# Half of a query projection moved among the first attention heads, rotation by head pairs, and two conditioning chunks moved to GpSimd

## The reference

```python
mod = c_act @ ada_w + ada_b                       # 1024 x 6144 for each layer
sh1, sc1, g1, sh2, sc2, g2 = jnp.split(mod, 6, axis=-1)
h = modulate(rmsnorm(x, n1), sh1, sc1)
x = x + g1 * mixer(h)                             # layer 0: retention, layer 1: attention
h = modulate(rmsnorm(x, n2), sh2, sc2)
x = x + g2 * f(h)                                 # layer 0: SwiGLU, layer 1: experts
```

```python
proj = h @ w_qkv
q = axial_rope(rmsnorm(q, q_norm_g)); k = axial_rope(rmsnorm(k, k_norm_g))
o = softmax(q @ k.T * 128 ** -0.5) @ v            # per head
m = o @ w_out
```

## Time and profile before

| what | us |
|---|---|
| median of 3 runs | 1654.36 (1654.05 to 1655.42) |
| the profiled execution | 1656.82 |
| its span, first to last instruction | 1654.6 |
| TensorE busy in the span | 1563.3 |
| VectorE busy | 1362.7 |
| ScalarE busy | 978.9 |
| GpSimd busy | 151.7 |
| attention, from the last copied norm to the output projection's end | about 512 to 620 |
| expert passes | about 644 to 1654 |

### The profile page before, as it was taken

One profiled execution on the slowest core, in us unless ns is written; L12 is line 12 of the kernel. 1 busy time (PEld: TensorE's weight loads), 2 busy tenths in 40 slices (PEclk: granted clock), 3 DMA queues, 4 the chain that ended last, 5 costly groups with the idle time before them and its releaser, 6 DMA issues.

```text
span 1654.6 us, 20642 instructions
## 1 busy us (share of the span) xinstructions
PE 1563.3 (94%) x6848; PEld 1248.5 (75%) x6848; DVE 1362.7 (82%) x1076; ACT 978.9 (59%) x790; POOL 151.7 (9%) x146
## 2 busy tenths in 40 slices
PE   5999779899997689999999999999999999999996
PEld 4677547677776568887888888888888888888885
DVE  6799478877767767888888888888888888888987
ACT  3444523433433636677777677677667667677763
POOL 0399400000002001000000000000000000000000
PEclk8999989999998898999999999999999999999998
DMA  9799319698894325999999999999999999999993
GB/s 340 281 346 354 118 38 360 234 304 268 296 323 131 121 67 203 378 365 347 357 368 353 356 366 353 356 369 352 356 367 353 356 367 353 355 366 355 343 368 119
DMA packets 237789, 503.16 MB, mean 304 GB/s; under 512 B 15725, under 2 KB 38381, under 8 KB 237625
## 3 DMA queue, kind: packets, MB, share of 16 engines
q1 hardware_dynamic: 234704, 491.50, 82.8%
q0 software_dynamic: 2464, 9.09, 1.6%
q10 hardware_dynamic: 586, 2.11, 0.3%
HBM read 500.54 MB, written 2.11 MB: 304 GB/s over the span
## 4 chain that ended last, share of the span: by engine, by line
PE 90%; DVE 6%; ACT 1%; issue 1%; DMA 1%; SPq 0%; DVEq 0%; ACTq 0%
PE bank L1656 27%; PE bank L1657 27%; PE bank L1658 27%; PE bank L1984 1%; PE bank L1637 1%; PE bank L1746 1%; DVE lo L1032 1%; DMA xs<-in_x 1%; PE bank L1651 0%; DVE hs L1070 0%; PE bank L1642 0%; PE bank L1864 0%; PE bank L2008 0%; SPq L435 0%; PE bank L2007 0%
## 5 line engine op out<-in xcount | busy, mean ns | idle before, releaser
L1432 DVE TENSOR_TENSOR lo<-stage,hi 128x2048 fp32r<-128x2048 f32 x168 | 383.7, 2287 | 53.0 <-ACT hi L906 52.7
L906 ACT CAST hi<-stage 128x2048 fp32r<-128x2048 f32 x168 | 321.4, 1913 | 134.0 <-DMA stage<-in_l_moe_w_up 119.0
L1657 PE MATMUL bank<-lo,hg_hi 128*128 128x512 f32 x896 | 354.3, 395 | 0.0
L625 ACT CAST hi<-stage 128x2048 fp32r<-128x2048 f32 x75 | 143.2, 1912 | 146.9 <-PE bank L1658 75.0
L1032 DVE TENSOR_TENSOR lo<-stage,hi 128x2048 fp32r<-128x2048 f32 x75 | 173.2, 2312 | 42.0 <-ACT hi L625 35.7
L1657 PEld LDWEIGHTS bank<-lo,hg_hi 128*128 128x128 f32 x896 | 168.8, 188 | 37.6
L1656 PE MATMUL bank<-hi,hT_hi 128*128 128x512 f32 x416 | 172.8, 415 | 10.0 <-DVE lo L1032 8.5
L1656 PE MATMUL bank<-hi,hg_hi 128*128 128x512 f32 x452 | 180.0, 398 | 0.2 <-issue 0.2
L1658 PE MATMUL bank<-hi,hg_lo 128*128 128x512 f32 x452 | 179.0, 396 | 0.0
L1657 PE MATMUL bank<-lo,eaT_hi 128*128 128x512 f32 x448 | 177.7, 397 | 0.0
L1657 PE MATMUL bank<-lo,hT_hi 128*128 128x512 f32 x416 | 167.5, 403 | 0.0
(11 more groups left out here) (291 smaller groups left out, 2703.2 us busy)
## 6 DMA issues: line engine op xcount, KB each, us to landing
stage<-in_l_moe_w_gate SPq DMA_DIRECT2D x224, 512.0 KB, 4.5
stage<-in_l_moe_w_up SPq DMA_DIRECT2D x224, 512.0 KB, 4.9
stage<-in_l_moe_w_down SPq DMA_DIRECT2D x224, 512.0 KB, 4.5
ada_w<-in_l_ada_w SPq DMA_DIRECT2D x40, 1024.0 KB, 5.3
stage<-in_l_ret_w_in SPq DMA_DIRECT2D x48, 512.0 KB, 7.5
stage<-in_l_ffn_w_gate SPq DMA_DIRECT2D x22, 512.0 KB, 7.6
stage<-in_l_ffn_w_up SPq DMA_DIRECT2D x22, 512.0 KB, 8.6
stage<-in_l_ffn_w_down SPq DMA_DIRECT2D x22, 512.0 KB, 7.6
```

Source lines behind the costliest of these rows:

```text
L625: nc.scalar.copy(hi[:, b % HRING, :], stage[:, b % RING, :]).then_inc(hi_done, 1)
L906: nc.scalar.copy(hi_e(b), stage[:, b % RING, :]).then_inc(hi_done, 1)
L1432: nc.vector.tensor_tensor(lo[:, b % RING, :], stage[:, b % RING, :], hi_e(b).bitcast(F32), ALU.subtract).then_inc(lo_done, 1)
L1657: mm(dst_ap, a_hi, w_lo, start=False, stop=False)
```

## The change

Five things:

1. The second query block (units 4 and 5 of the projection) is done by halves (`qkv_half`), with turns and the first scores between them. `head_rope` rotates two heads at a time. The heads 4 to 7 are rotated and turned among heads 0 to 3 of attention, with their own roots in that place.
2. `hi` of the output projection's weights goes to other buffers (`hi_o`), so that ScalarE and VectorE can prepare them earlier.
3. Chunks `A_AT` and `A_AT + 1` are added up by GpSimd (`ada_pool`), 16 instructions each: a multiply by the column into `ada_t`, and an add to `ada_acc`, each linked to the one before by a semaphore. They stand behind the fill of `moe` and ahead of the fetch for the second pass.
4. The load of chunk `A_AT + 1` stands behind the third round of expert loads in the first pass; before, it stood ahead of all expert loads.
5. The first pass's `middle` is written out on TensorE and ScalarE. TensorE's `ada_sum` of the two chunks stands after chunks 2 and 4, ScalarE's copies after its chunks 3 and 5.

```diff
-AQ_BANK = (7, 3, 7, 2, 7)
+AQ_BANK = (7, 3, 2, 3, 2)
...
+        def hi_o(k):
+            return (hi_h[:, :], hi_n[:, :], hi[:, 2, :], hi[:, 0, :])[k]
...
-            for half in range(2):
-                load_ada(A_AT + 1, half, l1_ada_w, l1_ada_b, (A_AT + 1 - A_L1) * AC)
...
-            chunks(0, 0)
+            chunks(0, 0, 1, 4)
+            for half in range(2):
+                load_ada(A_AT + 1, half, l1_ada_w, l1_ada_b, (A_AT + 1 - A_L1) * AC)
+            chunks(0, 0, 4, N_EC)
...
+            def ada_pool(c):
+                acc = ada_acc[:, c % 2, :]
+                for half in range(2):
+                    pool.wait_ge(a_load[half], (32, 16)[half] * (c + 1))
+                    if half == 0:
+                        pool.wait_ge(a_sum, c + 1)
+                    for j in range(AK):
+                        k = AK * half + j
+                        link(nc.gpsimd.tensor_scalar(ada_t[:, :], ada_w[:, half, j, :], cact[:, k:k + 1], None, ALU.mult))
+                        ins = nc.gpsimd.tensor_tensor(acc, ada_t[:, :], acc if k else ada_b[:, :], ALU.add)
...
+            ada_pool(A_AT)
+            ada_pool(A_AT + 1)
...
             for h in range(AH):
                 pT_take(h)
+                if h in (1, 3):
+                    aq_take(3 + h // 2)
                 if h:
                     o_take(h - 1)
+                if h == 0:
+                    qkv_squares(2)
+                if h == 1:
+                    head_roots(2)
...
             low(U_QKV + 1)
-            ada(A_AT, 0)
             low(U_QKV + 2)
-            ada(A_AT, 1)
             low(U_QKV + 3)
...
-            qkv_unit(4)
-            pe.wait_ge(arope, 2)
-            pe.wait_ge(a_out, 1 + A_AT + 1)
+            qkv_half(4, 0)
             aq_turn(1)
-            pe.wait_ge(aq_out, 1)
-            aq_turn(2)
-            qkv_unit(5)
-            pe.wait_ge(aq_out, 3)
+            qkv_half(4, 1)
+            pe.wait_ge(sq_done, 2 * TT)
+            pe.wait_ge(aq_out, 2)
             a_scores(0)
             a_scores(1)
-            pe.wait_ge(arope, 3)
-            aq_turn(3)
-            aq_turn(4)
+            aq_turn(2)
+            qkv_half(5, 0)
+            qkv_half(5, 1)
...
-            middle(0)
+            for j in range(2, N_EC - 1):
+                chunk(U_MOE - 2 + 6 * j, j, 0)
+                if j == 2:
+                    pe.wait_ge(put_done, 1)
+                    ada_sum(A_AT)
+                if j == 4:
+                    ada_sum(A_AT + 1)
+            pe.wait_ge(a_out, 1 + A_END)
```

More of the change, by code:

```diff
@@ L497, in load_down, with chunks @@
                          md_v[bass.ds(e, 1), :, ks, :].rearrange("a p k n -> p (a k) n"), more)
-            def chunks(e, more):
-                with sp.Fori(1, N_EC) as j:
+            def chunks(e, more, first, last):
+                with sp.Fori(first, last) as j:
                     jm = j * 6 - 6
@@ L513, in _ @@
                 load_down(before, U_MOE + 2, 4 * (N_EC - 1), w * UNITS_ITEM)
[L514 removed]
+                chunks(e, w * UNITS_ITEM, 1, N_EC)
             last = sp.value_load(meta[0:1, bass.ds(passes - 1, 1)], min_val=0, max_val=E - 1)
@@ L979, in _ @@
             e_silu_step(1, RING + U_MOE + 6)
-            middle(0)
+            for j in (2, 3):
+                chunk(U_MOE - 2 + 6 * j, j, 0, 0)
+            ada_take(A_AT, mod_at((A_AT - A_L1) * AC))
+            for j in (4, 5):
+                chunk(U_MOE - 2 + 6 * j, j, 0, 0)
+            ada_take(A_AT + 1, mod_at((A_AT + 1 - A_L1) * AC))
             passes = act.value_load(meta[0:1, 2 * N_TAB:2 * N_TAB + 1], min_val=E, max_val=E + 3)
@@ L1377, in _ @@
             row_max(0)
+            row_max(1)
+            low_o(1)
+            row_norm(0)
+            row_norm(1)
+            low_o(2)
+            head_rope(4, 2, qtab, 3 * TT).then_inc(arope, 1)
+            row_max(2)
             head_sums(2)
[L1379 to L1380 removed]
+            row_max(3)
+            o_low(0)
             head_scales(2)
[L1382 to L1399 removed]
+            row_norm(2)
+            row_max(4)
+            o_low(1)
+            head_rope(6, 2, qtab, 3 * TT).then_inc(arope, 1)
+            row_norm(3)
+            row_max(5)
+            o_low(2)
+            scale(3, A_AT)
+            row_norm(4)
+            row_max(6)
+            o_low(3)
+            row_norm(5)
+            row_max(7)
+            o_low(4)
+            low_o(3)
+            row_norm(6)
+            o_low(5)
+            dve.wait_ge(r_w, 1)
+            nc.vector.tensor_tensor(wr_hl[:, :, E:2 * E], wr[:, :, :], wr_hl[:, :, 0:E].bitcast(F32), ALU.subtract).then_inc(r_w, 1)
+            row_norm(7)
+            o_low(6)
+            o_low(7)
             def residual_tile(t):
@@ L1829, in qkv_unit, with qkv_half @@
                         kg == 0, kg == 1, 2 if k < 2 else None)
+            def qkv_half(k, t):
+                i, kg = k // 2, k % 2
+                h, l = unit(U_QKV + k, 4)
+                tok = slice(t * P, (t + 1) * P)
+                for j in range(4):
+                    ins = three(bank[:, QKV_BANK[i][t], :], hT_hi[:, 4 * kg + j, tok], hT_lo[:, 4 * kg + j, tok],
+                                h[:, j, :], l[:, j, :], kg == 0 and j == 0, kg == 1 and j == 3)
+                if t == TT - 1:
+                    ins.then_inc(w_used, 1)
             def aq_turn(i):
+                pe.wait_ge(arope, i + 1)
                 for k in range(2):
```

134 lines of the change are left out of this document (63 added, 71 removed).

## The result

The changed kernel takes 1666.78 us (median of 4 runs, 1665.83 to 1667.60), the kernel before 1654.89 (median of 4, the same chip). The ratio is 1.0071 with a 95% interval of 1.0056 to 1.0086: 12 us slower. The profiled executions differ by 10.2 us (span 1664.8 against 1654.6).

A forecast was written before the change was run, and what follows sets the result against it. TensorE was taken to bound the expert passes, VectorE's list attention. 1656.8 - 14 + 3 + 2 + 3 + 9 + 3 = 1662.8, less 2.5 is 1660.3, 1 off for overlap: 1659 us; range 1645 to 1668.

The forecast's parts named there:

- forecast case: First expert pass: GpSimd alternates with VectorE's splits and TensorE waits for it at the chunk sum; 1655 to 1664, chance 0.50.
- fourth rival: Attention wins only 9 us, and a multiply nearer 1.25 us makes the chunk sum 14 us late: 1667, chance 0.14.
- Attention: Attention stage up to the last head's turn: new order and VectorE's removed products win 14 us, bounds 9 and 17.
- The 4.8 us wait goes: Second query block: TensorE's wait for `lo` vanishes, so the projection ends at 550.8 instead of 556.4.
- First GpSimd chunk: Entry to the experts: four splits in a row, each later by nearly 1.0 us; 3 us lost (1 to 5).
- Moved load, and splits on the way: First expert pass: 2 us lost to displaced gate weights and their split, 3 us to slower splits up to chunk 4.
- The wait at the chunk sum: First expert pass, behind chunk 4: TensorE waits from 730.5 to 739.4 for GpSimd's second chunk, 9 us.
- one GpSimd instruction behind each split: First expert pass: GpSimd alternates with VectorE's splits; ten instructions at 2.2 + 1.0 us each take 32 us.
- GpSimd is in time: First expert pass: multiplies run beneath splits, GpSimd ends at 724 before TensorE needs the sum; 1647, chance 0.20.
- a short wait: Chunk sum: GpSimd ends between 731 and 735, TensorE waits 2 to 5 us; 1652 to 1656, chance 0.16.
- Slow clock behind the wait: After the idle stretch at the chunk sum TensorE starts at half speed, costing 3 us.
- The step to the median: Whole run: 2.5 us taken off, since the profiled run before lay that far above its median.

The follow-up runs named there:

- exp. 5: Kernel before with one line moved: TensorE's sum of the first chunk ahead of the second group's last QKV unit; 1649.7 us, ratio 0.9967.
- exp. 8: Old attention order, both chunks on GpSimd in the first expert pass with loads, sums and copies as in the changed kernel; 1671.7 us, ratio 1.0106.
- exp. 1: Changed kernel's attention order, both chunks back at their old places on VectorE with old loads, sums and copies; 1658.4 us, ratio 1.0019.
- exp. 6: New attention order, both chunks on VectorE, first chunk's sum moved ahead of the second group's last QKV unit; 1651.2 us, ratio 0.9974.
- experiment 7: New attention order, first chunk on VectorE with its sum moved earlier, second chunk's products on GpSimd during attention, no load moved; 1643.9 us, ratio 0.9931.
- experiment 4: New attention order, first chunk on VectorE, second chunk's products on GpSimd during attention, loads, sums and copies at old places; 1650.7 us, ratio 0.9976.
- Experiments 9: Kernel of experiment 7 plus 2 MB of conditioning weights loaded once more, unread, between third and fourth chunk of expert weights; 1647.7 us, ratio 0.9954.
- experiment 10: Kernel of experiment 7 plus GpSimd's 16 multiplies and 16 adds done once more from the router on, result unread; 1651.2 us, ratio 0.9975.
- experiment 3: Changed kernel with the load of GpSimd's second chunk one chunk of expert weights earlier in the queue; 1651.2 us, ratio 0.9979.

## Why the prediction came out as it did

The forecast case's mechanism happened: TensorE stood at the chunk sum until GpSimd was done. The direction is right and the time lies in the range, 7.8 us above the value given. But it is 2.8 above the bounds of the forecast case itself, 1655 to 1664, and stands at the fourth rival's 1667, whose late chunk sum came and whose loss in attention didn't. Terms of the sum are off both ways and cancel in part, and one reason is wrong. Of the signs named, the splits of 3.35 us, the two more table loads and the last turn near 51 us (50.2) are there.

**Attention: size right, reason mostly wrong.** Forecast 14 us, measured 15.3 from the key heads' turn to the last turn and 16.7 at the router's transposes, 1.2 of it an earlier start. The prediction gave it to the new order and to VectorE's two times 3.10 us of products. From key heads' turn to last turn the runs have:

| | both chunks on VectorE | on GpSimd, later |
|---|---|---|
| old order, late sum | 65.5 (before) | |
| old order, early sum or none | 56.2 (exp. 5) | 52.8 (exp. 8) |
| new order, late sum | 66.9 (exp. 1) | |
| new order, early sum or none | 56.5 (exp. 6) | 50.2 (changed kernel) |

Of the 15.3 us, 9.3 come from the first chunk's sum leaving the stretch in which ScalarE's copy blocked the casts, 3.4 from VectorE's missing products, and 2.6 from halves and pairs. That is one way through the table. With the products still on VectorE the new order gains nothing (56.5 against 56.2), and in the new order their going is worth 6.3. The step that failed is "The 4.8 us wait goes, since nothing stands between the casts of the last query weights and their products". The wait did go, but what had stood there was the copy of a sum. Reading only TensorE's waits, I saw `lo` as the releaser and did not follow it back to ScalarE's queue. That the size fits all the same is luck. (TensorE's terms up to the projection's end add up to 15.4 us, so to 550.3 and not to 550.8; the rest goes on from 550.1.)

**First GpSimd chunk: 3 forecast.** TensorE waited 2.58 us for `eact` there. From the transposes to chunk 0's turn the lead shrank by 1.3 only, but that isn't the price. TensorE is busy all through the router, and its granted clock there differs between the kernels (windows as in rows 2; before, then experiment 7):

```profile
630.00:640.00 10.00, 10.00 (x50) 10.00 (x50) 6.85 (x23) 6.45 (x5) 1.80 (x1) 0.52 0.14 57
```

```profile
617.00:627.00 10.00, 10.00 (x76) 9.96 (x75) 6.85 (x23) 8.00 (x7) 1.80 (x1) 0.83 0.17 70
```

From the router's transposes to chunk 0's turn it takes 36.8 us before, 38.1 in the changed kernel (0.76 from 613 to 623 us), 39.6 in experiment 6, and 33.6 in experiments 4, 7 and 9, where GpSimd does only its fill in that stretch, as before, and the clock was 0.83. Against those the first chunk costs 4.5 us, and experiment 10 has 3.8. That the forecast 3 lies near is luck: the kernel before had the slower clock there. What sets it no run shows.

**Moved load, and splits on the way: 2 + 3 forecast, 3.9 measured** from chunk 0's to chunk 4's turn. Experiments 9 and 10 price bytes and arithmetic at 6.9 and 5.1 us on the way to chunk 5, each by itself. Against the same experiment 7 the changed kernel loses 4.5 + 3.9 = 8.4 and not 12.0, so they don't add up. It may be that while TensorE loses time to the one, the queues gain on it for the other; that is argued from the sums, not shown by itself.

**The wait at the chunk sum: 9 forecast, 19.7 measured.** This is the term that was mis-sized. In the prediction's frame, moved by the forecast's net lead of 11 us, GpSimd was to run from 689.9 to 728.4 and TensorE to be at the sum at 719.5. GpSimd started 3.7 us earlier, at 686.2, but needed 48.1 us instead of 38.5 and ended at 734.3; TensorE was there at 714.7. So 5.9 us are GpSimd's and 4.8 TensorE's. Two numbers failed:
- the multiply at 0.75 us, between bounds of 0.45 and 1.25: it takes 1.56 alone, outside both. A fill writes without reading, and an add of two inputs is another instruction; neither row bounds a product by a column.
- "one GpSimd instruction behind each split, and each split later by nearly one GpSimd instruction": the multiply let two splits pass, and one split in three was longer. So GpSimd lost more than forecast and VectorE less. The forecast's 3.25 us for each unit was 2.7 in the rows above (8.2 us for three splits).

The rivals go with it. A multiply waits for one or two splits before it gets going, so "GpSimd is in time" and "a short wait" failed by this. The Trainium skill (SBUF — State Buffer, "Who interferes with whom") says that a VectorE instruction with two inputs in SBUF and a GpSimd instruction that reads SBUF exclude each other, and that whoever issues first gets the ports. The trace agrees on the first in these rows (5.49 us for a multiply of 1.56) and not in the row of 650.62, which shared 1.4 us with a split. It agrees on the second only in part: the multiply was issued at 709.02, ahead of the split at 710.88, and ran behind it. The Trainium skill's GPSIMD Engine Reference ("3.1 Elementwise — side-by-side cycle accounting") has 769 ns for 512 elements at best; this product by a column took twice that.

**Slow clock behind the wait: 3 forecast, 1.5 left for it.** From chunk 4's turn to chunk 5's the kernel lost 22.3 us: the wait of 19.7, 1.0 for the sum's two products, which stood elsewhere before, and 1.5 else. The window above has the clock at 0.57.

**The step to the median.** I took 2.5 us off because the profiled run of before lay that far over its median. The profiled run of the changed kernel, 1666.69 us, lies at its own. The profiled runs differ by 9.9 us where the terms gave 5: that is 4.9 us of the 7.8, and this step is 2.5; the rest is rounding.

**The wait is the whole of the loss, and the rest wins little.** Without it, by an earlier load, the changed kernel is 0.2% faster than before (experiment 3); with GpSimd at work in attention and no moved load, 0.2% as well (experiment 4), and with the early sum besides, 0.7% (experiment 7).

## What to carry to other kernels

When an engine waits for a split or a cast, follow the releaser back to its own queue before you credit a new order with the gain: here a copy that waited 9.0 us for a sum was worth 5.5 us of the whole by one moved line, in a kernel with none of the change's larger edits. Place a side calculation by where its consumer stands as well as by where its engine is idle, and keep every instruction that waits for it behind the work that others need, on each queue it touches. Don't bound an unknown instruction by others of another form.

## What the runs showed of the hardware

- GpSimd, 128x512 in f32, alone: a product by a scalar from a column 1.56 us, the same product with the column repeated as a second input 1.04, an add of two inputs 1.26.
- GpSimd's product by a column that became ready in a split took 3.0 to 3.6 us when no second split followed at once and 5.6 when one did, whether `eact` came next (709.02) or a third split (650.62). An add took 2.5 us behind one split and held the next up by 1.07, but another let two splits pass (4.98 us at 636.48).
- With two-input instructions back to back on GpSimd, VectorE's one-input product 128x256 (two in 0.62 us) took 2.2 to 2.5 us for two. In experiment 7, with the product by a column in between, they took 0.85 to 1.45:

```profile
571.98 0.85 DVE L1419 TENSOR_SCALAR prob<-prob,asm 128x256 f32<-128x256 f32 x2
...
573.46 1.21 DVE L1411 SCALAR_TENSOR_TENSOR asm<-asm,ahs 128x2 f32<-128x2 f32 x1
...
576.62 1.45 DVE L1419 TENSOR_SCALAR prob<-prob,asm 128x256 f32<-128x256 f32 x2
```

- Even an instruction of two columns can wait for a whole GpSimd add: 1.21 us above, 0.16 elsewhere in that list. In the changed kernel's router six small VectorE instructions took 2.8 us more than in experiment 7, and one split 1.1 more. One of the six stood beside an add and took 1.14 us in place of 0.16; three stood beside a multiply and lost 0.3 to 0.4 each.
- TensorE, busy throughout in both, was granted 0.52 of its clock in the router before and 0.83 in experiment 7, and the stretch took 3.3 us less.
